# Eight of sixteen modulation chunks multiplied and summed on VectorE beside the MLP, instead of on TensorE

## The reference, cut to what matters

```python
s_lat = jax.nn.silu(c)
s_ctx = jax.nn.silu(c_ctx)
for l in range(DEPTH_2):
    shift, scale, gate = jnp.split((s_lat @ w_mod[l] + b_mod[l])[:, None, :], 3, axis=-1)
    shift_c, scale_c, gate_c = jnp.split(s_ctx @ w_mod[l] + b_mod[l], 3, axis=-1)
    hx = _rmsnorm(x, norm_g[l]) * (1.0 + scale) + shift
    hc = _rmsnorm(ctx, norm_g[l]) * (1.0 + scale_c) + shift_c
```

## Time and profile before

| | us |
|---|---|
| time, median of 3 runs | 2873.31 (2869.96 to 2874.58) |
| the profiled execution | 2869.93 |
| its span | 2868.1 |
| PE busy | 2779.2 (97%) |
| DVE busy | 1750.4 (61%) |
| ACT busy | 1311.2 (46%) |
| granted clock, mean | 0.993 of full speed |

### The profile page before, as it was taken

The page is one execution under the profiler, slowest core; times in us unless marked ns, Lnnn a source line. Parts: engine busy times, 40 slices in busy tenths (PEclk is TensorE's granted clock), DMA queues, the critical chain, the costliest instruction groups (busy, mean ns, idle before and its releaser), DMA issues.

```text
span 2868.1 us, 33133 instructions
## 1 busy us (share of the span) xinstructions
PE 2779.2 (97%) x13403; PEld 2181.4 (76%) x13403; DVE 1750.4 (61%) x2326; ACT 1311.2 (46%) x1913; POOL 312.1 (11%) x260
## 2 busy tenths in 40 slices
PE   4999899999989999999999999999999999999998
PEld 3777788888867777777777887887778788877786
DVE  3546546665546566665544575659886665688764
ACT  3444335554443334434443444544555454545553
POOL 1000100000013001000000020024200011321001
PEclk9999899999999999999999999999999999999999
DMA  6877565446577776676777656565445555554543
GB/s 213 289 247 281 170 225 185 155 170 221 194 267 257 271 235 235 246 246 219 269 262 238 249 203 224 198 237 170 150 133 181 208 183 190 185 165 133 170 175 125
DMA packets 292360, 600.34 MB, mean 209 GB/s; under 512 B 12483, under 2 KB 19211, under 8 KB 290033
## 3 DMA queue, kind: packets, MB, share of 16 engines
q1 hardware_dynamic: 278272, 545.69, 55.8%
q0 software_dynamic: 10960, 49.10, 4.7%
q10 hardware_dynamic: 2976, 3.45, 0.4%
HBM read 585.02 MB, written 13.17 MB: 209 GB/s over the span
## 4 chain that ended last, share of the span: by engine, by line
PE 89%; DVE 6%; DMA 2%; ACT 1%; issue 0%; POOL 0%; SPq 0%; DVEq 0%; ACTq 0%; POOLq 0%
PE ps L642 25%; PE ps L644 24%; PE ps L643 24%; PE ps L654 3%; DVE wlo L1800 2%; DVE bvx L2321 2%; DMA raw<-in_w_in_dram 2%; PE ps L815 1%; PE ps L1047 1%; PE ps L1065 1%; PE ps L621 1%; DMA raw<-in_mlp_w_dram 1%; PE ps L800 1%; PE ps L867 1%; ACT whi L1234 1%; PE ps L767 0%
## 5 line engine op out<-in xcount | busy, mean ns | idle before, releaser
L1800 DVE TENSOR_TENSOR wlo<-raw,whi 128x1024 fp32r<-128x1024 f32 x840 | 1036.6, 1258 | 773.8 <-ACT whi L1234 769.0
L1234 ACT ACTIVATE whi<-raw 128x1024 fp32r<-128x1024 f32 x840 | 868.1, 1050 | 1217.6 <-PE ps L644 798.4
L642 PE MATMUL ps<-whi,ay_hi 128*128 128x512 f32 x1728 | 687.8, 398 | 4.7 <-DVE ay_lo L2287 2.4
L644 PE MATMUL ps<-whi,ay_lo 128*128 128x512 f32 x1728 | 674.0, 390 | 0.0
L643 PE MATMUL ps<-wlo,ay_hi 128*128 128x512 f32 x1728 | 673.3, 390 | 0.0
L642 PE MATMUL ps<-whi,ax_hi 128*128 128x512 f32 (+1 forms) x1632 | 649.2, 398 | 9.8 <-DVE wlo L1800 7.4
L644 PE MATMUL ps<-whi,ax_lo 128*128 128x512 f32 (+1 forms) x1632 | 634.1, 389 | 0.0
L643 PE MATMUL ps<-wlo,ax_hi 128*128 128x512 f32 (+1 forms) x1632 | 633.3, 388 | 0.0
L642 PEld LDWEIGHTS ps<-whi,ax_hi 128*128 128x128 f32 x1632 | 307.5, 188 | 115.7 <-issue 42.6
L642 PEld LDWEIGHTS ps<-whi,ay_hi 128*128 128x128 f32 x1728 | 324.7, 188 | 83.0 <-issue 12.1
L644 PEld LDWEIGHTS ps<-whi,ay_lo 128*128 128x128 f32 x1728 | 324.3, 188 | 69.1
(11 more groups left out here) (475 smaller groups left out, 2013.2 us busy)
## 6 DMA issues: line engine op xcount, KB each, us to landing
raw<-in_w_in_dram SPq DMA_DIRECT2D x208, 1024.0 KB, 5.1
raw<-in_mlp_w_dram SPq DMA_DIRECT2D x128, 1024.0 KB, 6.7
raw<-in_w_mod_dram SPq DMA_DIRECT2D x96, 1024.0 KB, 7.4
raw<-in_w_out_dram SPq DMA_DIRECT2D x64, 1024.0 KB, 5.1
raw<-in_ple_gate_dram SPq DMA_DIRECT2D x16, 1024.0 KB, 5.1
z2c<-zsc POOLq DMA_DIRECT2D x13, 512.0 KB, 3.2
h<-in_x_dram POOLq DMA_DIRECT2D x2, 2048.0 KB, 10.3
G<-bias_d ACTq DMA_DIRECT2D x4, 768.0 KB, 6.5
```

Source lines behind the costliest of these rows:

```text
L642: mm(dst, hi_[:, kk, tt], whi[:, x.s % 2, k, 0:w], start=(nth == 0), stop=False)
L644: ins = mm(dst, lo_[:, kk, tt], whi[:, x.s % 2, k, 0:w], start=False, stop=(nth == KT - 1))
L1234: A(whi[:, x.s % 2, 2 * kh:2 * kh + 2, 0:w], raw[:, x.slot, 2 * kh:2 * kh + 2, 0:w], ACT.Copy).then_inc(hi_ready, 1)
L1800: V.tensor_tensor(wlo[:, x.s % 2, ks, 0:w], raw[:, x.slot, ks, 0:w], f32v(whi[:, x.s % 2, ks, 0:w]), ALU.subtract).then_inc(lo_ready, 1)
```

## The change

Layer 1's eight shift and scale chunks (32 units, now the phase `modq`) are no longer multiplied by TensorE. VectorE does it: for each of the unit's four pieces it multiplies 128x512 of `raw` with the column of `c` and adds to one accumulator, and the same with `c_ctx` and the other, 8 instructions a unit. After four units TensorE multiplies each accumulator's four blocks of 128 columns with a column of ones, which sums over the rows. The gates of both layers (8 chunks, phase `modr`) stay on TensorE as they were. All is laid out anew: from n = 12 on, in eight groups of 14 MLP units, with the TensorE units after the group's MLP units 1, 3, 6 and 9 and the VectorE units in the list after 0, 4, 8 and 11. `modulation` is called two MLP units later. The slot of such a unit is given back by `mod_summed`. The load and transposes of `p` (`prow`), whose room the accumulator takes, come after the MLP.

```diff
-MODB = [(0, MODSS + i) for i in range(MODCH - MODSS)] + [(1, i) for i in range(MODCH)]
+MODR = [(0, MODSS + i) for i in range(MODCH - MODSS)] + [(1, MODSS + i) for i in range(MODCH - MODSS)]
+MODQ = [(1, i) for i in range(MODSS)]
+R_AT = [[12 + 14 * a + i for i in (1, 3, 6, 9)] for a in range(8)]
+Q_AT = [[12 + 14 * a + i for i in (0, 4, 8, 11)] for a in range(8)]
...
+            acc_b = sb("acc_b", [P, CH], F32, st)
+        accq = [zst[:, 1, TB], acc_b[:, :]]
...
         for n in range(128):
-            order += ["mlp"] + (["mod1"] if n < 7 * len(MODB) and n % 7 in (0, 1, 3, 4) else [])
+            order += ["mlp"] + ["modr"] * (n in sum(R_AT, [])) + ["modq"] * (n in sum(Q_AT, []))
...
-                        sp.wait_ge(plain_used, prev.p + 1)
+                        if prev.ph.name == "modq":
+                            sp.wait_ge(ev("mod_summed"), UPC * prev.i + prev.u + 1)
+                        else:
+                            sp.wait_ge(plain_used, prev.p + 1)
...
-                m_, at = n // 7, n % 7
-                if m_ < len(MODB) and at in (0, 1, 3, 4):
-                    if at == 0 and m_:
-                        pe.wait_ge(ev("modc_set"), MODSS + before(COLS, m_))
-                        pe.wait_ge(ev("mod_row"), before(ROWS, m_))
-                    mod_products(MOD1[4 * m_ + (0, 1, 0, 2, 3)[at]], 3)
-                elif m_ < len(MODB) and at == 5:
-                    pe.wait_ge(ev("modp_in"), MODSS + m_ + 1)
-                    if m_ in COLS:
-                        mod_columns(modp_b, 3)
-                    else:
+                a, at = (n - 12) // 14, (n - 12) % 14
+                if 0 <= a < len(MODR):
+                    if n in R_AT[a]:
+                        if at == 1:
+                            pe.wait_ge(ev("modc_set"), MODSS + a)
+                        mod_products(MODR_U[UPC * a + R_AT[a].index(n)], 3)
+                    if at == 10:
+                        pe.wait_ge(ev("modp_in"), MODSS + a + 1)
                         mm(ps[0:2, 3, :], sel[:, :], modp_b, start=True, stop=True).then_inc(ev("modc_sum"), 1)
+                    if at == 13:
+                        pe.wait_ge(ev("mod_row"), a + 1)
+                        pe.wait_ge(ev("mod_summed"), UPC * a + UPC)
+                        for j in range(4):
+                            for v in range(2):
+                                ins = mm(ps[:, 3, 2 * j + v:2 * j + v + 1], accq[v][:, j * P:j * P + P], ones[:, 0:1],
+                                         start=True, stop=True)
+                        ins.then_inc(ev("modc_sum"), 1)
...
+                a, at = (n - 14) // 14, (n - 14) % 14
+                if 0 <= a < len(MODR):
+                    if at == 9:
+                        mod_part(MODSS + a, MODR_U[UPC * a + 3], modp_b, 3)
+                    if at == 11:
+                        mod_row(a)
...
+            def modulation(y):
+
+                dve.wait_ge(raw_in[y.slot], y.landed)
+                if y.u == 0 and y.i:
+                    dve.wait_ge(ev("modc_sum"), MODSS + 2 * y.i)
+                for k in range(UK):
+                    w = raw[:, y.slot, k]
+                    for v in range(2):
+                        c_ = cvec[:, UK * y.u + k, v:v + 1]
+                        if y.u + k == 0:
+                            ins = V.tensor_scalar(accq[v], w, c_, None, ALU.mult)
+                        else:
+                            ins = V.scalar_tensor_tensor(out=accq[v], in0=w, scalar=c_, in1=accq[v], op0=ALU.mult, op1=ALU.add)
+                        if v:
+                            link(ins) if k < UK - 1 else ins.then_inc(ev("mod_summed"), 1)
...
                 beside(n - 2)
-                if n % 7 == 1 and n // 7 - 1 in COLS:
-                    mod_set(1, MODB[n // 7 - 1][1], MODSS + n // 7)
+                for a in range(len(MODQ)):
+                    if n - 2 in Q_AT[a]:
+                        modulation(MODQ_U[UPC * a + Q_AT[a].index(n - 2)])
+                if n >= 28 and (n - 28) % 14 == 0:
+                    a = (n - 28) // 14
+                    mod_set(1, MODQ[a][1], MODSS + 2 * a + 2)
```

More of the change, by code:

```diff
@@ L352, in build @@
             Phase("mlp", None, 0, 8 * FF_Q, 2, "kept"),
-            Phase("mod1", None, 0, len(MODB), 1, "modb", split=False),
+            Phase("modr", None, 0, len(MODR), 1, "modb", split=False),
+            Phase("modq", None, 0, len(MODQ), 1, "modb", split=False),
             Phase("pp", None, 0, 4, 2, "pp", split=False),
@@ L422, in laid @@
                     a_ += 2
-                out_.append(Unit(ph, k // UPC, k % UPC, r_, s_ if ph.split else None, None if ph.split else p_, a_))
-                s_, p_ = s_ + (1 if ph.split else 0), p_ + (0 if ph.split else 1)
+                plain = not ph.split and name != "modq"
+                out_.append(Unit(ph, k // UPC, k % UPC, r_, s_ if ph.split else None, p_ if plain else None, a_))
+                s_, p_ = s_ + (1 if ph.split else 0), p_ + (1 if plain else 0)
             return out_
@@ L545, in build @@
         for n in ("vec_T", "vec_cols", "cvec_ready", "bias_out", "lam_dot", "lam_exp",
[L546 removed]
+                  "mod_summed", "mod_row", "modp_in", "modc_sum", "modc_set", "x_again", "post_sq", "post_g", "rms_sum", "rms_root",
                   "pT_psum", "pT_ready", "p_in", "h_in", "lru_w", "bd_zero",
@@ L579, in _ @@
                 elif x.ph.kind == "modb":
-                    l, col = MODB[x.i]
+                    l, col = (MODR if x.ph.name == "modr" else MODQ)[x.i]
                     sp.dma_start(raw[:, x.slot], w_mod[l][:, UK * x.u:UK * x.u + UK, col * CH:col * CH + CH])\
@@ L1173, in _ @@
                 hand_unit(x, AX_ if x.ph.name in ("out2_0c", "out2_0", "in2_1x") else AY_)
+                if n == 2:
+                    pe.wait_ge(ev("p_in"), 16)
+                    pe.wait_ge(ev("modc_set"), MODSS + len(MODQ))
+                    for k in range(2):
+                        for b in range(TB):
+                            ins = nc.tensor.transpose(ps[:, 3, (k * TB + b) * P:(k * TB + b + 1) * P],
+                                                      prow[:, b, k * P:k * P + P], eye[:, :])
+                    ins.then_inc(ev("pT_psum"), 1)
                 if 3 <= n < 7:
@@ L1567, in _ @@
                     hT_part(x.i // 8 * 4 + x.i % 8 - 1)
-                if n % 7 == 6 and n // 7 < len(MODB):
-                    mod_part(MODSS + n // 7, MOD1[4 * (n // 7) + 3], modp_b, 3)
-                if n % 7 == 1 and n // 7 - 1 in ROWS:
-                    mod_row(n // 7 - 1)
+                a, at = (n - 14) // 14, (n - 14) % 14
[4 more added lines that the diff above has]
+                        mod_row(a)
                 if n % 4 == 2 and x.i > 28:
@@ L2586, in _ @@
                         .then_inc(ev("e_in"), 16)
-                for m_ in ROWS:
-                    if i == (7 * m_ + 8) // 4 + 1:
-                        l, col = MODB[m_]
-                        k = before(ROWS, m_)
-                        pool.wait_ge(ev("mod_row"), k + 1)
-                        dma(mod_d[l][:, col * CH:col * CH + CH], modst_b[:, k % 2, :]).then_inc(mod_out[k % 2], 16)
+                for a, (l, col) in enumerate(MODR):
+                    if i == (12 + 14 * a + 12) // 4 + 1:
+                        pool.wait_ge(ev("mod_row"), a + 1)
+                        dma(mod_d[l][:, col * CH:col * CH + CH], modst_b[:, :]).then_inc(mod_out[0], 16)
                 if i % 8 < 4:
@@ L2599, in _ @@
                 context(i)
-            for zp in range(2):
-                pool.wait_ge(mod_out[zp], 16 * len(ROWS) // 2)
+            pool.wait_ge(ev("modc_sum"), MODSS + len(MODR) + len(MODQ))
+            dma(prow, I["p"][0, 0].rearrange("(b p) n -> p b n", p=P)).then_inc(ev("p_in"), 16)
+            pool.wait_ge(mod_out[0], 16 * len(MODR))
             ctx_loads(0)
```

39 lines of the change are left out of this document (13 added, 26 removed).

## The result

| | before | with the change |
|---|---|---|
| time, median | 2871.64 us | 3025.09 us (3021.7 to 3031.73) |
| ratio | 1 | 1.0527 [1.0511, 1.0543] |
| span of the profiled execution | 2868.1 | 3029.9 |

The change makes the kernel 5.3% slower: 153 us on the medians, 162 on the two spans. The direction and the mechanism are those of the prediction; the size is three times what its sum gave (+51), and lies outside its range.

What follows compares the result with a forecast made beforehand. It took TensorE's own work as the bound, with the weight ring full and hidden by a margin. -33 + 6 + 70 + 14 - 6 = +51 us on 2869.9 gave 2921, or 2924 on the median; range 2882 to 2972.

Steps and rivals of the forecast that it cites:

- the rejection of VectorE as the bound for good: In the MLP, VectorE's added 179 us were said to fit into its some 297 idle us.
- the rival in which the margin holds: VectorE reaches the modulation units early enough, the ring hides the late release: 2840 us, faster; chance 0.11.
- Removed, added on TensorE, the start: -33, +6, -6: On TensorE: 32 units' products gone, -33 us; doubled column-sum matmuls, +6; idle time and slow matmuls at the MLP's start, -6.
- VectorE's 5.6 us a unit: On VectorE, a modulation unit's eight 128x512 instructions were to take 5.6 us, 179 us in all.
- The waits: +70: TensorE's waits in the MLP from late slots: 8.8 us a group, 8 groups, +70 us; bounds 36 and 123.
- I take the short landing, since the queue is empty when such a load leaves.: Late MLP loads were taken to land in 5.05 us, not the median 6.7.
- The prediction's other end: Loads landing in 6.7 us make the MLP's waits 123 us; as a rival 2977 us, chance 0.13.
- The release 8.1 us after n0's end: VectorE was to finish the modulation, called behind hand_low of unit n0+2, 8.1 us after MLP unit n0's end.
- The margin of 6.0: At one place read in the MLP, a unit's weights were ready 6.0 us before TensorE got there.
- Who waits: 24 TensorE waits of 2.6 to 3 us: products of unit 1 (modc), MLP units 7 (wlo), row sum (modp_b).
- The clock: +14, between 0 and 43: Every third of 24 TensorE waits drops the clock, 8 x 1.8 us for nine slow matmuls: +14 us.
- The rival in which each wait drops the clock: Every MLP wait starts TensorE at half clock, clock term 43 us instead of 14: 2953 us, chance 0.18.

Runs made afterwards that it cites:

- The tiny version at its early place: The changed kernel with modulation called one MLP unit earlier and multiply-adds cut to 8 of 512 columns: 2835.78 us, ratio 0.9868 against the kernel before.
- the quarter version: The changed kernel, modulation at the same place, with multiply-adds covering 128 of 512 columns: 2914.79 us in one run.

## Why the prediction was wrong in its size

**What bounds the kernel** was right: the ring is full all the time, and the change lengthens the time that a slot is held. So was the rejection of VectorE as the bound for good (63% busy), and the rival in which the margin holds fell: VectorE's idle time stands ahead of the modulation in its queue. In the earlier trace rows it stands before a step of the attention, `cst`, that waits for TensorE, and the `hand_low` comes only behind that; the text had it before the `hand_low` itself. (VectorE's room was counted over 690 us; the 112 MLP units from unit 12 on take 774 at 6.91 each, so there was more.)

**Removed, added on TensorE, the start: -33, +6, -6.** Right. The tiny version at its early place has them without the waits: -36 us. From start to start the column sums (L1016) take 13.6 us in all, where the kernel before had eight chunks at 0.81: +7. The idle 4.69 us at the start are gone.

**VectorE's 5.6 us a unit.** Right: 5.2 us for a chunk's first unit and 5.8 for the others in the trace after. The rows of a multiply-add are 0.75 us long with starts 0.67 and 0.78 apart in turn.

**The waits: +70.** This is the step that failed. Adding up the idle time in front of TensorE's rows from 800 us to the end of the MLP gives 137.9 us, and 10.4 in the kernel before: +127.5. The 10.4 hold the 4.7 us at the start that are gone, so the waits themselves are +132, where the prediction had +70. Three parts of the step were too small.
- *"I take the short landing, since the queue is empty when such a load leaves."* It isn't. A late release frees the loads behind it too; SP's rows at 1669.16 to 1670.12 show three within 1 us, and the first took 6.4. The landings of L594 in 900:1800 show it as a whole:

```profile
DMA to landing us min/median/max: 5.0/7.8/14.6
```

  The load that waits for the slot, that of n0+3, took 5.9 us in the median of its 24 places, 5.1 to 8.0. Those behind it pay more: of 177 loads of SP in 850:1800, 31 left with three others still on their way and took 11.8 us in the median; in the kernel before, of as many from 850 us to the MLP's end, it was one. The prediction's other end, 6.7 us a load from the earlier trace rows, gave 123 us. That this is near the 132 is partly luck, since it held the release at 8.1. (The fit of the Trainium skill, DMA: Bandwidth & Descriptors, Anatomy of one DMA, that the prediction gave beside this is one for transfers that GpSimd issues. SP issues these, and the shortest in the earlier trace rows took 5.0 us.)
- *The release 8.1 us after n0's end.* It is 10.3 in the median. The weight halves ahead of the modulation end 4.0 us after n0's end in the median and not 2.5, and steps of `context` come between. In the first unit of a group they are later still, 7.4 us in the mean, where the quarter version has 4.7: there one late release makes the next one later. In the other three the two versions are alike (3.1 to 4.1 and 3.2 to 4.4), so this feedback is a part of the loss and not all of it. The margin of 6.0 that all this was taken from was sound: from a load's landing, with 2.3 us for its first weight half, to the start of its unit on TensorE, the kernel before has 6.0 us in the median of the 48 places where the slot goes to an MLP unit, though under 5.2 in a quarter of them.
- *Who waits.* The places were foreseen for the most part: the products behind unit 1 waited 37.6 us for `modc` in seven waits (predicted 2.9 each, measured 5.4), and the row sum 41.2 in eight, seven of them in the window above (2.9 against 5.2, behind the copy that stands behind the late halves and one more copy that I had left out). What I had not counted is the attention: `ce`, four waits, 17.1 us. VectorE does it behind the late weight halves and the taps:

```profile
1175.30 2.36 DVE L1812 TENSOR_TENSOR wlo<-raw,whi 128x1024 fp32r<-128x1024 f32 x2 [7.43 <-ACT whi L1245]
1177.58 1.67 DVE L2162 SCALAR_TENSOR_TENSOR cbv<-cuc,cols,cbv 128x256 f32<-128x256 f32 x4
...
1179.61 0.48 DVE L2172 SCALAR_TENSOR_TENSOR ce<-ce,cst 128x256 f32<-128x256 f32 x1
```

  There are 37 waits over 0.3 us instead of 24, and 18 of them are over 3.5 us. (One of these, 4.6 us for POOL at the start of the MLP, was there before.)

**The clock: +14, between 0 and 43.** Also mis-sized, and beyond its bound. I compared each distance between two starts on TensorE in the MLP, less idle time, with the median distance of the same kind of row before. Over the distances at the half clock the surplus is 51 us if none may more than double, and 65 if those count whole that are longer, as where a row is missing; before it was 4. So the clock is +47 to +61. The prediction put every third wait at a drop, since its waits of 2.6 to 3 us lay nearer the row without one. The waits became longer, and of the 18 over 3.5 us every one has a granted clock under 1.00 in the 5 us behind it, of the 19 shorter ones six. And a drop costs more than the 1.8 us of nine matmuls: behind the wait of 7.28 us the row sum, at 1679.08, takes 0.85 us more than at full clock, and the matmuls behind it come 0.43 apart until 1683.60. That is some 2.3 us; 47 to 61 us over 24 drops are 2.0 to 2.5 each.

```profile
1679.00:1684.00 5.00, 4.92 (x10) 2.59 (x11) 2.93 (x4) 2.03 (x3) 0.00 (x0) 0.51 1.05 389
```

That window is granted 0.51, the level of 1.2 GHz. The rival in which each wait drops the clock was thus right for long waits. The Trainium skill (TensorE: Matmul & The Clock Gate, HAM oscillation) describes bursts of matmuls with waits for data between them, each of which starts at the half clock. The trace after agrees at its long waits, while behind ten of the 14 waits under 2.5 us the clock stays at 1.00.

**The sum with the measured terms:** -33 + 7 + 127.5 + 47 to 61 = +148.5 to +162.5 at the end of the MLP, where 163.4 are lost (the 6 us of the start lie in the idle time and the surplus). Up to 15 us are not placed. The step to blame is that of the waits: it is 62 of the 112 us by which the sum was short. The clock's term is 33 to 47 more, and follows from the waits' length.

## What to carry to other kernels

When work that holds a ring's slot moves to another engine, ask first behind which instruction of that engine's queue it stands and when the slot comes back, not how many us the engine has free: the same 179 us of VectorE work gave 3025 or 2849 us by the place of its call. A release worked out from one quiet place comes too early; read where the work ahead of it ends over all places (here 4.0 us and not 2.5), take the landing of loads that leave in bursts, and look for places where one late release stands ahead of the next. Work that returns a resource goes as early as its inputs allow, and is cut in pieces where something else that is waited for stands behind it.

## What the runs showed of the hardware

- A multiply-add (SCALAR_TENSOR_TENSOR) of 128x512 in float32 with an accumulator takes 0.75 us, and back to back 0.67 to 0.78; the plain multiplication with a column (TENSOR_SCALAR, L2232) of the same size is shorter:

```profile
1127.92 0.48 DVE L2232 TENSOR_SCALAR zst<-raw,cvec 128x512 f32<-128x512 f32 x1
```

- The landing of a 1 MB load goes with how many of SP's loads are still on their way when it leaves. In the trace after, in 850:1800, the medians are 5.5 us with none (36 loads), 7.5 with one (47), 9.1 with two (63) and 11.8 with three (31); before they are 5.3, 7.2 and 8.6 for none to two. The windows of this MLP show the DMA engines only 49 to 61% busy: the average says nothing about loads that leave in bursts.
